# Filler matmuls moved from the units of a chunked scan into its opening, and their operands reread in eight pieces

## What is computed

```
h   = RMSNorm(x) * g1 * (1 + scale1) + shift1
mix = W_o( sigmoid(gate_a) * W_pa(GQA(h)) + sigmoid(gate_b) * W_pb(BiGatedDeltaNet(h)) )
x   = x + gate1 * mix
x   = x + gate2 * SwiGLU(RMSNorm(x) * g2 * (1 + scale2) + shift2)

BiGatedDeltaNet: 8 heads of 64, gated delta rule
  S_t = a_t (I - b_t k_t k_t^T) S_{t-1} + b_t k_t v_t^T,  o_t = S_t^T q_t
  one forward and one backward scan, outputs summed
```

## Time and profile before

| what | value |
|---|---|
| timed runs | 2967.61, 2967.79, 2977.02 us; median 2967.79 |
| the profiled execution | 2968.09 us, its span 2966.3 us |
| TensorE busy | 2681.6 us, 90% of the span |
| VectorE, ScalarE, GpSimd busy | 47%, 35%, 20% |
| the projection's last matmuls end at | about 550.5 us |
| the scan | from about 554 us to about 1254 us |
| first matmuls of unit 0 | 610.37 us |

### The profile page before, as it was taken

How to read it: one execution, slowest core, us unless ns; L and a number is a source line. 1 busy time by engine, 2 the same in 40 slices (tenths; PEclk the granted TensorE clock), 3 DMA queues, 4 the chain that set the end, 5 groups by cost and what they waited for, 6 DMA issues and landing times. The chain is left out here.

```text
span 2966.3 us, 46114 instructions
## 1 busy us (share of the span) xinstructions
PE 2681.6 (90%) x18134; PEld 2525.5 (85%) x18134; DVE 1400.3 (47%) x2320; ACT 1040.5 (35%) x1801; POOL 606.5 (20%) x489
## 2 busy tenths in 40 slices
PE   7999999589898999828999869989999999999999
PEld 3898999578888888726777758889999999999999
DVE  3565331157666766447888833352222242222222
ACT  4312332233343333136778733322222222222211
POOL 1001222434333433143323221210111000111100
PEclk9999999779897999858999979999999999999999
DMA  5324664334343433140000044332222233222232
GB/s 202 144 80 131 220 220 153 101 91 111 100 151 80 122 85 86 59 163 14 9 17 16 12 181 166 116 99 71 78 78 71 78 114 94 71 78 72 69 96 70
DMA packets 194779, 294.22 MB, mean 99 GB/s; under 512 B 82704, under 2 KB 121648, under 8 KB 192816
## 3 DMA queue, kind: packets, MB, share of 16 engines
q1 hardware_dynamic: 191728, 276.15, 29.6%
q10 hardware_dynamic: 2880, 15.73, 1.5%
HBM read 228.28 MB, written 63.52 MB: 98 GB/s over the span
## 5 line engine op out<-in xcount | busy, mean ns | idle before, releaser
L277 PE MATMUL f_ps<-mf_h_hi,mf_w_hi 128*128 128x320 f32 x1408 | 435.1, 309 | 1.4 <-PEq L1982 1.4
L277 PE MATMUL f_ps<-mf_h_hi,mf_w_lo 128*128 128x320 f32 x1408 | 435.1, 309 | 0.0
L277 PE MATMUL f_ps<-mf_h_lo,mf_w_hi 128*128 128x320 f32 x1408 | 435.1, 309 | 0.0
L2415 DVE TENSOR_TENSOR mf_w_lo<-mf_w_raw,mf_w_hi 128x1024 fp32r<-128x1024 f32 (+1 forms) x135 | 188.8, 1399 | 431.6 <-ACT mf_w_hi L2267 431.4
L277 PE MATMUL proj_ps<-h_hi,w_hi 128*128 128x320 f32 x896 | 282.7, 316 | 6.0 <-DVE w_lo L575 5.6
L277 PE MATMUL proj_ps<-h_hi,w_lo 128*128 128x320 f32 x896 | 278.0, 310 | 0.0
L277 PE MATMUL proj_ps<-h_lo,w_hi 128*128 128x320 f32 x896 | 278.0, 310 | 0.0
L277 PEld LDWEIGHTS f_ps<-mf_h_hi,mf_w_hi 128*128 128x128 f32 x1408 | 264.4, 188 | 1.6 <-issue 1.6
L277 PEld LDWEIGHTS f_ps<-mf_h_lo,mf_w_hi 128*128 128x128 f32 x1408 | 264.4, 188 | 0.0
L277 PEld LDWEIGHTS f_ps<-mf_h_hi,mf_w_lo 128*128 128x128 f32 x1408 | 264.4, 188 | 0.0
L2341 POOL TENSOR_TENSOR f_ff_lo<-f_ff_f,f_ff_hi 128x640 f32 (+1 forms) x44 | 69.3, 1576 | 783.1 <-ACT f_ff_hi L2267 783.1
(11 more groups left out here) (323 smaller groups left out, 6425.2 us busy)
## 6 DMA issues: line engine op xcount, KB each, us to landing
mf_w_raw<-w_up_dram SPq DMA_DIRECT2D x88, 512.0 KB, 3.5
w_ada_raw<-w_ada_dram SPq DMA_DIRECT2D x16, 1024.0 KB, 5.2
mf_w_raw<-w_mix_dram SPq DMA_DIRECT2D x32, 512.0 KB, 5.0
w_raw<-w_in_dram SPq DMA_DIRECT2D x28, 512.0 KB, 5.1
mf_w_raw<-w_down_dram SPq DMA_DIRECT2D x32, 448.0 KB, 3.3
delta_t<-delta_tile ACTq DMA_DIRECT2D x10, 1024.0 KB, 6.7
fill_raw<-w_in_dram SPq DMA_DIRECT2D x20, 512.0 KB, 4.2
kq_t<-delta_t SPq DMA_DIRECT2D x20, 512.0 KB, 4.3
```

Of the source, the lines that this page charges most:

```text
L277: ins = nc.tensor.matmul(out, w(k), a(k), start=(first and n == 0 and q == 0), stop=(last and n == len(ks) - 1 and q == 2))
L2415: nc.vector.tensor_tensor(wlo[:, slot, 0:nk], raw[:, slot, 0:nk], whi[:, slot, 0:nk].bitcast(F32), ALU.subtract).then_inc(E[half]["lo"], 1)
```

## The change

The plan of the fillers (`quota`): six a slot in units -3 and -2, twelve in unit -1 (78 + 78 + 156 = 312 in the opening, where 52 were), three a slot from unit 0 on (39 a unit, where 52 were), until the first half is through in unit 4 (12); none in units 5 and 6; three a slot again from unit 7 to 18, and 12 in unit 19. The total stays 960.

The first weight tile of the fillers is loaded and split, and the second loaded, by the last turns of the projection, in the projection's own buffers `w_raw`, `w_hi`, `w_lo`, which now live on through the scan and take the place of `fill_raw`, `fill_hi`, `fill_lo`. To make room, buffers of the first stage lie in others: `mod_rows` in `w_raw` (so the first weight loads now wait for `cols_done`), the two bg operands in `w_lo`, their rows in `x`.

SP's program at the scan's start loads the decay rows and k, q of units 0 to 2 first, the masks in between. `x_base` is cleared by VectorE and not by GpSimd. TensorE's waits for `eyes_ready` and `zeroed` move to unit 0, VectorE's to unit -2.

`h_late` is read back in eight DMAs of two k slices of the high or low part each (`reload`), at four places of units 5 and 6, where it was two DMAs at the end of the first half (unit 8). The second half's first filler waits for all eight.

```diff
-        def plan(u, s, quota):
-            got = []
-            t, i = divmod(at[0], PER)
-            n = min(quota, 3 * KT - i % (3 * KT))
...
+        RELOAD = 5
+
+        def quota(u):
+            if u < 0:
+                return 12 if u == -1 else 6
+            return 3 if u < RELOAD or u >= RELOAD + 2 else 0
 
         for u in UNITS:
             for s in range(SLOTS):
-                plan(u, s, 4 if -1 <= u < NT - 1 or u >= NT else 0)
...
+                t, i = divmod(at[0], PER)
+                n = min(quota(u), 3 * KT - i % (3 * KT))
+                pieces[u, s] = []
+                if n and t < (FILL_TILES if u < RELOAD else NF):
+                    pieces[u, s] = [(t, i // (3 * KT), i % (3 * KT), i % (3 * KT) + n)]
+                    at[0] += n
...
+            def reload(u, i):
+                if u in (RELOAD, RELOAD + 1):
+                    n = 4 * (u - RELOAD) + i
+                    ks = slice(2 * (n // 2), 2 * (n // 2) + 2)
+                    if n == 0:
+                        sp.wait_ge(e["fill_ps"], 2 * FILL_TILES)
+                    sp.dma_start((h_hi, h_lo)[n % 2][:, ks].bitcast(F32), io["h_late"][n % 2][:, ks]).then_inc(e["h2_in"], 16)
...
-                        if t == FILL_TILES - 1:
-                            sp.dma_start(h_hi[:].bitcast(F32), io["h_late"][0]).then_inc(e["h2_in"], 16)
-                            sp.dma_start(h_lo[:].bitcast(F32), io["h_late"][1]).then_inc(e["h2_in"], 16)
...
+            load_rows(0)
+            load_kq(0)
             for name in ("offdiag", "levels"):
                 sp.dma_start(keep[name][:], io[name]).then_inc(e["masks_in"], 16)
-            load_weights(0)
-            load_weights(1)
+            load_rows(1)
+            load_kq(1)
+            load_kq(2)
...
+                reload(u, 0)
                 for s in range(0, 3):
                     fill(u, s)
...
+                reload(u, 1)
...
+                reload(u, 2)
                 if has(u - 1):
                     store(u - 1)
...
                 if has(u + 2):
                     blocks_in(u + 2)
+                reload(u, 3)
```

More of the change, by code:

```diff
@@ L68, in ada_and_norm @@
         c_raw = sb("c_raw", [P, KT, 2])
[L69 to L73, removed]
+        rows = keep["w_raw"][0:2].rearrange("p t k n -> p (t k n)")
         hf = sb("h_f32", [P, HR, 3 * P])
+        bg_raw = hf[:, HR - 1, 0:KT * 32].rearrange("p (k n) -> p k n", k=KT)
+        bg_hi, bg_lo = (keep["w_lo"][:, p, 0:2].rearrange("p k n -> p (k n)").rearrange("p (k n) -> p k n", k=KT) for p in range(2))
+        bg_t = lambda b: x[0:32, TAPS[b][0], 0:span(b)[1] - span(b)[0]]
         sq = hf[:].rearrange("p r n -> p (r n)")[:, 0:D]
@@ L225, in _ @@
                 for j in range(*TAPS[b]):
-                    last = nc.tensor.transpose(col_ps[:, 32 * j:32 * j + 32], bg_t[:, j * P:(j + 1) * P], keep["ident"][0:32, 0:32])
+                    last = nc.tensor.transpose(col_ps[:, 32 * j:32 * j + 32], bg_t(b)[:, (j - TAPS[b][0]) * P:(j - TAPS[b][0] + 1) * P], keep["ident"][0:32, 0:32])
             last.then_inc(bg_cols, 1)
@@ L799, in delta_scan @@
         o_stored = [sem(f"o_stored{i}") for i in range(2)]
-        fw_in = [sem(f"fill_in{i}") for i in range(2)]
+        fw_in = keep["w_in_sems"]
         f_stored = [sem(f"fill_stored{i}") for i in range(2)]
@@ L937, in _ @@
                     sp.dma_start(S[half(h), 1, d, :, h], io["state_in"][d, half(h)]).then_inc(e["state_in"], 16)
-            sp.wait_ge(e["xb_zero"], 1)
             for u in UNITS:
-                if has(u + 3):
-                    if u < 0:
-                        load_kq(u + 3)
+                if has(u + 3) and u >= -1:
                     load_rows(u + 3)
+                reload(u, 0)
                 for s in range(0, 3):
@@ L956, in _ @@
                     inverse_out(u + 1)
+                    if u == -1:
+                        sp.wait_ge(e["xb_zero"], 1)
                     inverse_in(u + 1)
+                reload(u, 1)
                 if u == 4:
@@ L1334, in _ @@
             for u in UNITS:
+                if u == 0:
+                    pe.wait_ge(e["eyes_ready"], 2)
+                    pe.wait_ge(e["zeroed"], 4)
                 body(u)
@@ L2553, in build @@
         }
+        keep["w_in_sems"] = [ctx.enter_context(nc.semaphore(f"w_in{p}")) for p in range(2)]
         keep["first_sem"] = ctx.enter_context(nc.semaphore("first_sem"))
@@ L2563, in build @@
                 keep["c_act"] = c1.enter_context(nc.sbuf_tensor("c_silu", [P, KT, 2], F32))
-                keep["w_raw"] = c1.enter_context(nc.sbuf_tensor("w_raw", [P, 2, KT, P], F32))
-                keep["w_in_sems"] = [c1.enter_context(nc.semaphore(f"w_in{p}")) for p in range(2)]
                 keep["b_ada"] = c1.enter_context(nc.sbuf_tensor("b_ada_sb", [P, 48], F32))
```

57 lines of the change are left out of this document (22 added, 35 removed).

## The result

| | kernel before | changed kernel |
|---|---|---|
| median of 20 runs each, us | 2967.7 | 2974.4 |
| ratio to before, 95% interval | 1 | 1.0029 (1.0020 to 1.0038) |
| span of the profiled execution, us | 2966.3 | 2968.2 |

The forecast was 2952 us, with a range of 2922 to 2980. The changed kernel is not 0.5% faster, as forecast, but about 0.3% slower: inside the range, on the other side of the kernel before.

What follows compares the result with a forecast made beforehand. The longer of TensorE's stream (28.3 us) and the diagonal blocks' turn (about 30) was taken to set each unit. Terms of -5.5, -9.6, 0 and -1 sum to -16, from 2968.1 to 2952 us, range 2922 to 2980.

Steps and rivals of the forecast that it cites:

- The opening's matmuls: Opening: 312 fillers, mostly at the full level, and k, q products sum to 59.9 us; with waits, unit 0 starts at 618.
- The waits put at 4 us: Opening: waits of copies out of the fillers' bank in ScalarE's order, between 0 and 8 us, taken as 4.
- The rival that the opening stays at the half level: Opening: its fillers run at 0.267 us each, so it ends 36 us later; total 2993 us, chance 0.06.
- Unit 0 and the start of unit 1: Opening and unit 0: unit 0 starts 7.5 us later but runs faster, unit 1's matmuls start at 641; together 5.5 us gained.
- no longer leads there: Opening: the diagonal blocks' way no longer sets unit 0's start, though blocks_out of unit 0 goes at 582 to 587.
- Thirteen units at 28.5: Units 1 to 3 and 8 to 17: 28.5 us each plus clock falls, 396.5 in all, 9.6 less than before.
- five units with a fall of the clock: Units 1 to 3 and 8 to 17: five have a pause past 1.8 us, each costing 5.2 us.
- The rival that waits of 1.4 us bring the clock down in every unit: Units 1 to 3 and 8 to 17: all 13 have falls, 438 us, +32; total 2997 us, chance 0.12.
- Units 4 to 7: Units 4 to 7: 29.5, 35.5, 31.5 and 36.5 us, together 133, no change; from 125 to 141.
- that stays: Units 4 and 5: SP's wait for the fourth unit's state and its store ahead of blocks_out remain; unit 5 takes 35.5 us.
- -5.5, -9.6, 0 and -1: Forecast changes in us: opening with unit 0, the thirteen units, units 4 to 7, and unit 18 and after.
- the line by length: TensorE's pauses: one between 1.1 and 1.8 us is where a unit gets 6 to 7 us longer.

Runs made afterwards that it cites:

- e4: The changed kernel with filler weight tile 2 loaded first and state_out moved to unit 5 behind its load of keys and values; 2967.1 us, ratio 1.0001.
- e6: e4 with the eight pieces of h read earlier, four behind blocks_in of unit 4 and four behind that of unit 5; 2957.4 us, ratio 0.9976.
- e1: The changed kernel with the load of filler weight tile 2 issued first in SyncE's queue of the scan, ahead of 13 DMAs; 2970.5 us, ratio 1.0023.
- e2: The changed kernel with the fillers' plan of the kernel before, pieces of h read in unit 9; 2961.4 us, ratio 0.9982.
- e3: The kernel before with state_out and its wait moved from unit 4 to unit 5, behind the load of keys and values; 2953.6 us, ratio 0.9963.
- e5: e1 with the 312 opening fillers at other places: 120 in unit -3, none in -2, 192 in -1; 2975.7 us, ratio 1.0036.
- e8: e2 with state_out in unit 5 and pieces of h earlier, six at the end of unit 8, two in unit 9; 2940.0 us, ratio 0.9912.
- e9: e8 with 156 first-half fillers drawn from units 5 to 8 into units -3 and -2, six a slot; 2961.1 us, ratio 0.9990.
- e11: e8 with 12 fillers a slot instead of 4 in unit -1 and 3 instead of 4 in units 0 to 8; 2942.5 us, ratio 0.9929.
- e7: e6 with the opening's fillers placed as in e5; 2967.6 us, ratio 1.0002.
- e10: e6 with four fillers a slot instead of three from unit 7 on; 2956.9 us, ratio 0.9985.
- e12: e8 with all pieces of h read in unit 8 and 28 second-half fillers already in unit 9; 2942.6 us, ratio 0.9928.

## Why the prediction was wrong, step by step

**The opening's matmuls: right but for one wait.** The fillers ran at the full level and the opening ended at 622.7, with 618 forecast. The waits put at 4 us had a single one of 3.99 in them, and TensorE ran 3.4 us at the half level behind it. The rival that the opening stays at the half level, 36 us longer, did not come. The Trainium skill ("TensorE: Matmul & The Clock Gate", section "A second HAM failure mode: psum-queue depth-cycling") tells of a kernel that cycles through banks and whose clock goes back and forth over short idle times between groups. The trace does not show that for this kernel: its groups follow each other in one bank, with seven such pauses between 578 and 620, at 1.00.

**Unit 0 and the start of unit 1: the step that failed.** The prediction held that the diagonal blocks' way "no longer leads there". It set the second blocks_out by TensorE's stream, at 609.5, put the first at 582 to 587 and named no loss from it, and so had unit 1's first matmuls at 641. They came at 651.2, its first y_res at 651.8. The second blocks_out stands in SP's queue behind inverse_in of the first turn, and it was issued at 616.39, a turn of 29.2 us behind the first at 587.24, not at 609.5. Before, the two were 26.8 us apart (582.09 and 608.91). Where the units start follows the first blocks_out. Unit 1's own start moves with unit 0's clock: e4 and e6, the same program up to unit 4, have it at 648.2 and 643.8. Unit 2's, one turn later, is the steadier mark:

| kernel | first blocks_out | unit 1 starts | unit 2 starts | from blocks_out to unit 2 |
|---|---|---|---|---|
| before | 582.1 | 647.9 | 676.7 | 94.6 |
| changed | 587.2 | 651.8 | 683.3 | 96.1 |
| load first (e1) | 581.6 | 647.7 | 680.4 | 98.8 |
| plan of before (e2) | 571.9 | 634.0 | 666.1 | 94.2 |
| before, state_out moved (e3) | 580.7 | 640.2 | 677.2 | 96.5 |
| other places, unit 0 at 1.00 (e5) | 583.3 | 650.2 | 686.0 | 102.7 |
| fastest (e8) | 572.1 | 634.8 | 666.8 | 94.7 |
| e8 with the opening's fillers (e9) | 587.1 | 649.8 | 683.6 | 96.5 |
| unit -1 filled (e11) | 572.9 | 644.4 | 671.8 | 98.9 |

The traces that the table leaves out give 98.9 (e4), 97.5 (e6), 103.6 (e7), 98.7 (e10) and 94.0 (e12). So unit 2 starts 94 to 99 us after the first blocks_out, except in e5 and e7, whose slots have up to 24 fillers: 103.

So the opening was never idle time to be filled. It was two turns in a row, with TensorE waiting for them. The new frame starts the first turn 10.2 us sooner, a gain that the prediction left out; the 260 added fillers take 15.3 away again. 5.7 of these are the late load (e1). The other 9.7 (571.9 in e2, 581.6 in e1) are the work put ahead of tile 0's products and copies; whether it is TensorE's part or ScalarE's that counts was not separated, since e5 took it from TensorE's unit -2 and ran into ScalarE's queue instead. e8 and e9, which differ by 156 of these fillers and where they were taken from, show both parts together, 15.0. The lines of e5 and e11 say what many fillers in unit -1 do: they lengthen the turns themselves.

**Thirteen units at 28.5: right in the sum, by luck.** They took 398.2 us, with 396.5 forecast and 406.1 before. The forecast was 28.5 for a clean unit and five units with a fall of the clock, over 33 us each. Only one is over 33 us, unit 11 with 36.0; the other twelve take 28.6 to 32.6, 30.2 on average. And the sum hides two parts. Units 1 to 3 lost 3.3. Units 8 to 17 gained 11.2: units 10 and 14, which had falls before and have none now, gave 14.4, unit 11 took 5.6, and unit 8, which the reading of h left, gave only 1.3. The rival that waits of 1.4 us bring the clock down in every unit came in part and cheaply: of the ten waits of 1.37 to 1.39 us ahead of bank A products in these units, four are followed by some 3.5 us at the half level (as at 727.56), six by none (as at 697.78).

Three fillers a slot in place of four went with 7.9 us more over eight units in one pair of kernels (e6, e10) and 11.2 less over seven in another (e11, e8), and neither pair's medians differ clearly. A clean unit is a turn long, 29 to 30 us, and what fillers do beyond that they do through the clock; that reading rests on e9's units without fillers and is not shown for 39 against 52.

**Units 4 to 7: "that stays".** Forecast 133, measured 137.6. Unit 4 took 34.7 where 29.5 was forecast, units 5 and 6 35.7 and 35.8 for 35.5 and 31.5, unit 7 31.5 for 36.5. Of unit 4's 5.2 us too many, e6 and e10 show that one execution has them and another not. The prediction took unit 5's wait behind state_out as given. It was the dearest single wait that was tested: one block moved in SP's queue made the kernel before 0.37% faster, where the whole change was forecast at 0.53%. The wait at unit 7's first filler was foreseen at 5 us; in the changed kernel it was 0.55, but in e1, e4 and e5, which reach it sooner, it was 6.74, 3.74 and 6.71, with the half level behind it.

**The sum.** Forecast -16.1 from -5.5, -9.6, 0 and -1; the traces show +3.9, -7.9, +4.4 and -0.1, together +0.3. Of the 16.4 us between them 9.4 are the start of unit 1, 4.4 units 4 to 7, 1.7 the thirteen units, 0.9 the end of the scan. The medians put the whole change at +6.7. Where the other 6.4 lie, one trace of each kernel can't show, and that stays open; units of one program differ by as much between executions (unit 4 in e6 and e10).

## What to carry to other kernels

An engine that idles in a stretch does not make the stretch a place for more work: first follow what the stretch waits for, and count for each added instruction which queues its loads, splits and copies stand in ahead of that chain. If work is moved out of full units, ask what then keeps the clock up in them. Before a difference of a few us between two traces is put down to an edit, look at a stretch where both run the same program. And when a gain vanishes, look for the next wait on something with a fixed arrival, here the pieces of h: remove that first, and then see what the change was worth.

## What the runs showed of the hardware that was not expected

The length of a pause alone does not say whether the granted clock falls. In e6 a pause of 1.25 us ahead of the y_res products is followed by 9 us at half level, and one of 1.41 us ahead of a later level's bank A products by nothing. TensorE's rows and the stretches behind them:

```profile
970.50 0.47 PE L1212 MATMUL banks_bc<-y_res,x_inv 128*128 128x128 f32 x1 [1.25 <-DVE y_res L1176]
...
1070.28 1.32 PE L1212 MATMUL bank_A<-x_inv,n_t_eye 128*128 128x128 f32 x8 [1.41 <-DVE attn_t L1136]
```

```profile
1066.00:1078.00 12.00, 10.32 (x77) 8.72 (x76) 9.10 (x16) 9.73 (x18) 1.28 (x1) 1.00 0.32 88
971.00:980.00 9.00, 9.00 (x38) 7.82 (x39) 6.18 (x12) 4.68 (x9) 1.22 (x1) 0.50 0.07 16
```

The changed kernel has the first kind too, 1.28 us at 981.62, with TensorE at 0.50 from there to 995 and unit 11 at 36.0 us. But the kind does not decide either. Another wait for y_res of the changed kernel, in unit 2, was longer, and the clock stayed at the full level:

```profile
692.26 0.33 PE L1210 MATMUL banks_bc<-y_res,x_inv 128*128 128x128 f32 x1 [1.66 <-DVE y_res L1174]
692.00:727.00 35.00, 30.90 (x239) 28.18 (x239) 26.31 (x51) 14.69 (x24) 12.08 (x10) 1.00 0.34 89
```

The prediction had drawn the line by length, between 1.10 and 1.77. The runs give no rule to put in its place: the pauses differ in what stands around them, and none of these kernels changed that alone. In e1 a wait of 1.07 us for y_res at 980.95 is followed by 13 us at 0.50.

A fall can cost more than the pause. In e4 3.74 us of waiting were followed by 22 us at 0.50, and unit 7 was 40.7 us in place of 31.5 in the changed kernel. How much it costs is not fixed by the pause: the 2.39 us in unit 4 of e6 were followed by some 3 us at 0.50, the 2.38 us at the same place of e10, in the same program, by 17.
